# Convolution banks evicted whole and placed by transfers, a one-step candidate in the bisection, and a denser plan of its rounds

## The chip, the core and the metric

One core of a Trainium2 chip runs the whole program. The metric is device time in microseconds of one execution; a kernel is timed by the median of several executions.

## The reference, cut to what matters

The program is one layer of a decoder over 1024 tokens of width 1024. One input projection `x @ w_in` is split by columns into the inputs of three mixers that run side by side:

- sparse attention: a light indexer (8 heads of 32) scores every key for every query, `sum over h of relu(iq_h . ik) * iw_h`; each query keeps its 256 best keys, and softmax attention runs over those;
- a pooling mixer: trailing means over 2, 4, 8 and 16 positions minus the token, then a small linear map;
- a convolution module on 256 channels: `h = a * sigmoid(gate)`, a causal depthwise convolution of width 31 plus bias, a LayerNorm over the 256 channels, then silu.

```python
h = a * jax.nn.sigmoid(gate)
h = lax.conv_general_dilated(h, conv_w, window_strides=(1,), padding=[(CONV_WIDTH - 1, 0)],
                             feature_group_count=D_C, ...) + conv_b
h = layer_norm(h, ln_g, ln_b)
return jax.nn.silu(h)
```

The three outputs are joined, projected with `w_o`, normalised, and pass through a grouped mixture of experts (16 experts, two per token) and a second norm.

## The kernel before, in words

**Stages.** The span has these stretches: load and transposes of x with the first projection units (to about 49 us), the indexer (to about 119), the bisection for the 256th best score (to about 234), attention (to about 396), the output projection, norm and routing (to about 520), the experts, and the last norm.

**Projection units.** The list `UNITS` holds 33 projection units (index 0 to 32), 8 `key` units and 8 `val` units. A projection unit of 512 columns is 24 matmuls (L472 to L474), with operands split into a high and a low part. ACT evicts most units (`unit` in the scalar block, L1047 on); ACT also makes the high part of the next weight tile (L1036), and DVE the low part (L1386, `w_split`). Banks are reused every fourth unit.

**Indexer.** From unit 8 (`kv`) on, PE issues `IDX_PER_UNIT` = 6 score products between the matmuls of each projection unit (`index`, L719 to L733); ACT applies relu (L1090), and DVE adds the eight heads up in `bias` (L1446, L1449) and takes the largest magnitude of a block (L1453). There are 48 products, so units 8 to 18 carry them; unit 18 (`gate0`, second half) carries the last three. The products read `stack_iq` and `stack_ik`, which are put together by transfers: SP issues 4 for `stack_ik` and 8 for the high part of `stack_iq` (L555, behind a wait on DVE's low part of unit 3), and ACT issues 8 for its low part (L1108), each of 96 KB. PE waits for all of them before product 0 (L723).

**Bisection.** 25 rounds. In each, DVE counts the scores below a candidate in blocks 7, 6 and 2 (L1502) and ACT in blocks 5, 4 and 3 (L1119). DVE then forms `passed` (L1517), `spot` (L1519) and the next candidate (L1520); at the head of the next round it forms `floor` (L1497). Both engines take, between their counts, the remaining projection units off a list (`in_round`: 7 units in 10 rounds, unit 19 to 32 in rounds 1 to 19); DVE's part is `w_split` and, for `a0`, the product with the sigmoid (L1432). In the four rounds after these DVE builds the banded weights of the convolution (`toep`, L1511), and ACT evicts two `key` or `val` units in a round.

**Convolution.** The first 128 channels go to PE. Their input is held by time modulo 4 (`phased`), and 16 transfers (L574) stack it. A bank of 256 columns for each of four groups of 32 channels takes `SPAN` = 9 matmuls (L763); `CONV_PER_UNIT` = 3 of them stand before each unit from `CONV_FROM` = 37 on. In a bank, partition 32q + c holds channel c of the group at phase q. `conv_out` (L1123 to L1128) evicts each bank with four ACT instructions of 32x256, which move the phases to the group's 32 partitions and write every fourth element, so that `conv[:, 0, :]` comes out in the order of time. The other 128 channels are done by POOL, tap by tap (L1938 to L1952), from the moment the last `a0` unit is done.

**Attention.** The order of steps is computed by `attention_steps()`. The first scores need all `key` and `val` units evicted (L794 on, `unit_act`); the second pair needs the bisection's end. Two pool matmuls (L851) wait for all of `conv0`. Near its end stand the LayerNorm steps of the convolution: means (`cm`, L857), subtraction (L1614), squares (L1211), variance (L863), scaling (L1623), silu (L1155). The step `split 0` on ACT and the `cm` step on PE wait for POOL's last tap.

Of the kernel before, what the change touches and what calls it, by code (L numbers as in the profile page):

```python
# [71 lines left out]
CONV_PER_UNIT = 3  # L72
IDX_PER_UNIT = 6
# [137 lines left out]
def program(nc, a):  # L211
    ctx = ExitStack()
    with ctx:
# [37 lines left out]
        stack_h = at("stack_h", [P, PHASES, 264], F32, CC)  # L251
        toep_w = at("toep_w", [P, PHASES, 4 * SPAN], F32, CC + 4.25)
# [142 lines left out]
        spot, floor, thr = (ps[:, 3, 8 * i:8 * i + 6] for i in range(3))  # L395
# [31 lines left out]
        toep_in, phased_in = sem("toep_in"), sem("phased_in")  # L427
# [67 lines left out]
        CONV_FROM = PROJECTIONS + 4  # L495
# [14 lines left out]
        def in_round(r):  # L510

            return (r + 1) * 7 // 10 - r * 7 // 10
# [5 lines left out]
        def _(sp):  # L518
# [43 lines left out]
            sp.wait_ge(unit_dve, seen(BY_DVE, UNITS.index(("iq0", 1, 1))))  # L562
# [101 lines left out]
        def _(pe):  # L664
# [88 lines left out]
            def conv_part(n):  # L753
# [14 lines left out]
            for k, between in PLAN[1:]:  # L768
                if k >= CONV_FROM:
                    for n in range(CONV_PER_UNIT):  # L770
                        conv_part((k - CONV_FROM) * CONV_PER_UNIT + n)
# [9 lines left out]
            for step in STEPS:  # L781
                kind = step[0]
                if kind in RING:
                    r = step[-1]
                    out = ps[:, 4 + (r + 2) % 3, :]
                    if r in (1, 2):
                        pe.wait_ge(conv0, PHASES * PHASES)
# [243 lines left out]
        def _(act):  # L1031
# [1081 lines left out]
```

## Time and profile before

| what | us |
|---|---|
| median of 3 executions | 994.54 (991.64 to 996.25) |
| the profiled execution | 993.15 |
| its span in the profile | 991.4 |
| PE busy in the span | 892.1 (90%) |
| DVE busy | 689.7 (70%) |
| ACT busy | 570.5 (58%) |
| POOL busy | 344.9 (35%) |

A row of the timeline gives start, duration, engine, line, operation, output and inputs, shape and count, and in brackets the idle time of the engine before it and who ended that. The chain of waits follows back, from the last instruction, what each piece of work waited for; it lists start, length and work. PE's durations are modelled with a pipelined end, so two matmuls in a row overlap; the distance of their starts, which the chain shows, is what each costs.

### The profile page before, as it was taken

Reading aid. Unit: us, or ns where it says so; the run is one execution under the profiler, and the core shown is the slowest. Engines: PE = TensorE matmul, PEld = TensorE weight load, DVE = VectorE, ACT = ScalarE, POOL = GpSimd, SP = SyncE. Lnnn points to the kernel's source line nnn. Section 1 sums busy time; section 2 is a strip of 40 time slices with the busy share of each in tenths; the row PEclk is TensorE's granted clock in tenths of the full one; section 3 lists DMA queues with packets and bytes.
Section 4 is the critical chain, followed back from the end, with each engine's and each line's share of the span. In section 5 each row is a group of like instructions: output and inputs, shape, how many; then the busy total and the mean of one; then the engine's idle time right before and its main releaser. Section 6 shows DMA issues by size and latency. Waiting matters only on the chain.

```text
span 991.4 us, 15972 instructions
## 1 busy us (share of the span) xinstructions
PE 892.1 (90%) x4780; PEld 714.1 (72%) x4781; DVE 689.7 (70%) x1060; ACT 570.5 (58%) x820; POOL 344.9 (35%) x264
## 2 busy tenths in 40 slices
PE   6999989888899899999918999999999999999980
PEld 5778868655466567888816888888878888888760
DVE  5478799994789945737687757888888854234276
ACT  5276567678787665702233647778777743324342
POOL 0000059999999940000001112132332321111137
PEclk9989989999899999999968999999999999999995
DMA  8731022000000100433576779999999987652475
GB/s 229 189 78 43 22 65 86 1 1 1 1 1 2 43 2 23 152 132 123 229 286 225 248 229 339 380 403 388 397 404 385 400 295 243 185 148 44 108 243 211
DMA packets 64254, 173.08 MB, mean 175 GB/s; under 512 B 19553, under 2 KB 34401, under 8 KB 51888
## 3 DMA queue, kind: packets, MB, share of 16 engines
q1 hardware_dynamic: 56048, 143.61, 39.2%
q0 software_dynamic: 7488, 27.07, 11.1%
q10 hardware_dynamic: 672, 1.84, 0.5%
q8 instruction: 24, 0.39, 0.2%
q14 instruction: 22, 0.18, 0.1%
HBM read 142.79 MB, written 26.74 MB: 171 GB/s over the span
## 4 chain that ended last, share of the span: by engine, by line
PE 59%; DVE 17%; DMA 11%; issue 6%; ACT 5%; ACTq 1%; DVEq 0%; POOLq 0%; POOL 0%; SPq 0%
PE ps L472 14%; PE ps L474 14%; PE ps L473 14%; DMA raw<-in_w_gate 10%; DVE junk_dve L1502 6%; PE ps L806 3%; PE ps L836 3%; PE ps L823 2%; DVE wlo L1809 2%; PE ps L962 2%; PE ps L731 1%; DVE sm L1655 1%; ACT whi L1280 1%; PE ps L763 1%; ACT junk_act L1119 1%
## 5 line engine op out<-in xcount | busy, mean ns | idle before, releaser
L1809 DVE TENSOR_TENSOR wlo<-raw,whi 128x2048 fp32r<-128x2048 f32 x96 | 216.2, 2288 | 51.8 <-ACT whi L1280 51.8
L1280 ACT CAST whi<-raw 128x2048 fp32r<-128x2048 f32 x96 | 180.3, 1911 | 50.2 <-DMA raw<-in_w_gate 17.0
L472 PE MATMUL ps<-whi,xgT_hi 128*128 128x512 f32 x384 | 152.6, 397 | 6.2 <-DVE xgT_lo L1819 6.2
L474 PE MATMUL ps<-whi,xgT_lo 128*128 128x512 f32 x384 | 150.3, 392 | 0.0
L473 PE MATMUL ps<-wlo,xgT_hi 128*128 128x512 f32 x384 | 150.2, 391 | 0.0
L472 PE MATMUL ps<-xT_hi,w_hi 128*128 128x512 f32 (+1 forms) x224 | 89.7, 401 | 8.7 <-DVE w_lo L1386 6.9
L472 PEld LDWEIGHTS ps<-whi,xgT_hi 128*128 128x128 f32 x384 | 72.7, 189 | 22.3 <-issue 6.3
L473 PE MATMUL ps<-xT_lo,w_hi 128*128 128x512 f32 (+1 forms) x224 | 88.4, 395 | 0.0
L474 PE MATMUL ps<-xT_hi,w_lo 128*128 128x512 f32 (+1 forms) x224 | 88.4, 394 | 0.0
L2020 POOL COPY idx_now<-slot_token 128x1 int32 (+1 forms) x24 | 8.2, 343 | 219.3 <-PE ps L962 219.3
L474 PEld LDWEIGHTS ps<-whi,xgT_lo 128*128 128x128 f32 x384 | 72.5, 189 | 15.5
L473 PEld LDWEIGHTS ps<-wlo,xgT_hi 128*128 128x128 f32 x384 | 72.5, 189 | 14.3
L1119 ACT ACTIVATE junk_act<-bias,sm 128x768 bf16<-128x768 f32 (+2 forms) x75 | 62.2, 829 | 27.8 <-DVE sm L1520 25.8
L472 PE MATMUL ps<-whi,hT_hi 128*128 128x512 f32 x192 | 76.9, 401 | 0.5 <-issue 0.5
L1502 DVE TENSOR_SCALAR_CACHE_REDUCE junk_dve<-bias,sm 128x1024 bf16<-128x1024 f32 (+2 forms) x75 | 75.7, 1009 | 1.8
L474 PE MATMUL ps<-whi,hT_lo 128*128 128x512 f32 x192 | 75.1, 391 | 0.0
L473 PE MATMUL ps<-wlo,hT_hi 128*128 128x512 f32 x192 | 74.9, 390 | 0.0
L2035 POOL DMA_INDIRECT acc_d<-ysb,idx_add x23 | 40.6, 1763 | 92.8 <-ACT ysb L1307 91.9
L1590 DVE CUSTOM_DVE_ANT_0 probs<-ps,bias 128x128 f32<-128x128 f32 (+7 forms) x64 | 45.9, 755 | 36.0 <-PE ps L806 30.7
L1948 POOL TENSOR_SCALAR tapped<-hpad,par 128x512 f32<-128x512 f32 x32 | 58.3, 1833 | 0.1
L1297 ACT ACTIVATE silu<-ps 128x512 f32<-128x512 f32 x24 | 14.3, 596 | 76.5 <-PE ps L474 76.5
L472 PEld LDWEIGHTS ps<-xT_hi,w_hi 128*128 128x128 f32 x224 | 43.6, 195 | 18.9 <-issue 8.0
(335 smaller groups left out, 1874.4 us busy)
## 6 DMA issues: line engine op xcount, KB each, us to landing
raw<-in_w_gate SPq DMA_DIRECT2D x32, 1024.0 KB, 12.0
raw<-in_w_up SPq DMA_DIRECT2D x32, 1024.0 KB, 12.7
raw<-in_w_down SPq DMA_DIRECT2D x32, 1024.0 KB
w_raw<-in_w_in SPq DMA_DIRECT2D x14, 512.0 KB, 3.9
x_tok<-in_x SPq DMA_DIRECT2D x8, 512.0 KB, 7.8
wo_raw<-in_w_o SPq DMA_DIRECT2D x16, 256.0 KB, 2.9
x_res<-in_x SPq DMA_DIRECT2D x16, 256.0 KB, 3.5
x_d<-xa SPq DMA_DIRECT2D x4, 512.0 KB, 5.7
```

The costliest lines, as they stand in the source:

```text
L472: pe.matmul(out, l_hi, r_hi, start=start, stop=False)
L473: pe.matmul(out, l_hi, r_lo, start=False, stop=False)
L474: return pe.matmul(out, l_lo, r_hi, start=False, stop=stop)
L806: last = pe.matmul(scores_at(u + h, WIDTH[b])[:, c:c + n], qT[rows, j, b * P:(b + 1) * P], keyT[rows, j, c:c + n], start=True, stop=True)
L836: last = pe.matmul(product_at(pair_no)[h * HD:(h + 1) * HD, :], value[:, k, (2 * j + h) * HD:(2 * j + h + 1) * HD], pT[:, PT_NO[b, j, n] % ...
L1119: act.activation(junk_act[:, 0:WIDTH[b]], bias[:, AT[b]:AT[b] + WIDTH[b]], ACT.Sign, bias=cands[r % 2][:, c:c + 1], scale=-1.0, accum_out= ...
L1280: act.copy(whi[:, n, :], raw[:, n, :]).then_inc(gu_hi if n < 4 else dn_hi, 1)
L1502: dve.tensor_scalar(junk_dve[:, 0:WIDTH[b]], bias[:, AT[b]:AT[b] + WIDTH[b]], now[:, c:c + 1], 0.0, ALU.is_lt, ALU.add, accum_out=res[:, c ...
L1590: dve.tensor_tensor_reduce(out=probs_at(u)[:, 0:WIDTH[b]], in0=scores_at(u, WIDTH[b]), in1=bias[:, AT[b]:AT[b] + WIDTH[b]], scale=-1.0, sc ...
L1809: dve.tensor_tensor(wlo[:, n, :], raw[:, n, :], f32(whi[:, n, :]), ALU.subtract).then_inc(gu_lo if n < 4 else dn_lo, 1)
L1948: pool.tensor_scalar(tapped[:, half], src[:, half], by, None, ALU.mult).then_inc(tap_mul, 1)
L2035: pool.indirect_dma_start(acc_d, bass.IndirectOffsetOnAxis(ap=idx_add[:], axis=0), ysb[:], None, compute_op=ALU.add).then_inc(y_out, 16)
```

## The change

- Indexer: 7 products in a unit in place of 6, so that unit 17 carries the last three and unit 18 moves into the bisection. Of ACT's 8 transfers of the low part, 4 go to the POOL queue, with a semaphore of their own. SP's 8 transfers of the high part wait for ACT's eviction of unit 3, no longer for DVE's low part.
- Bisection: `floor` is carried from round to round, `spot` and the instruction L1497 go; the candidate is `(floor + step / 2) * top_score` in one instruction. Units are taken in 5 rounds of 6, so units 18 to 32 lie in rounds 1 to 17, `toep` in rounds 18 to 21.
- Convolution: 5 matmuls before each unit, from unit 41 on. One ACT instruction of 128x256 evicts a bank into `stepped`; 16 transfers on SP's queue, four for each bank, put it in place. `conv[:, 0, :]` is then held phase-major (all times of one phase together), and the LayerNorm's steps, the squares and the silu read or write it through a rearranged view.

```diff
-CONV_PER_UNIT = 3
-IDX_PER_UNIT = 6
+CONV_PER_UNIT = 5
+IDX_PER_UNIT = 7
...
+        stepped = at("stepped", [P, PHASES, 256], F32, R2 + 28)
...
-        CONV_FROM = PROJECTIONS + 4
+        CONV_FROM = PROJECTIONS + 8
+
+        def conv_ends(k):
+
+            return [g for g in range(PHASES) if (SPAN * (g + 1) - 1) // CONV_PER_UNIT == k - CONV_FROM]
+
+        def conv_at(i, c):
+
+            if i:
+                return conv[:, 1, c * 512:(c + 1) * 512]
+            return conv[:, 0, :].rearrange("p (r v) -> p v r", r=PHASES)[:, c * P:(c + 1) * P, :]
...
-            return (r + 1) * 7 // 10 - r * 7 // 10
+            return (r + 1) * 5 // 6 - r * 5 // 6
...
-            sp.wait_ge(unit_dve, seen(BY_DVE, UNITS.index(("iq0", 1, 1))))
+            sp.wait_ge(unit_act, seen(BY_ACT, UNITS.index(("iq0", 1, 1))))
             stack(0, range(2))
...
+            for g in range(PHASES):
+                sp.wait_ge(conv0, g + 1)
+                for q in range(PHASES):
+                    t0 = (PHASES - 1 - q) * 256
+                    sp.dma_start(conv[g * CH:(g + 1) * CH, 0, t0:t0 + 256], stepped[q * CH:(q + 1) * CH, g, :]
+                                 ).then_inc(phased_in, 16)
             sp.wait_ge(searched, 1)
...
-                    pe.wait_ge(stack_in[0], 16 * 20)
+                    pe.wait_ge(stack_in[0], 16 * 16)
+                    pe.wait_ge(stack_lo_in, 16 * 4)
...
-                        pe.wait_ge(conv0, PHASES * (g - 1))
+                        pe.wait_ge(conv0, g - 1)
...
                     pe.wait_ge(conv1, 2 * TAPS)
+                    pe.wait_ge(phased_in, 2 * 16 * PHASES * PHASES)
                     for i in range(2):
-                        last = pe.matmul(out, ones_conv[:], conv[:, i, c * 512:(c + 1) * 512], start=i == 0, stop=i == 1)
+                        last = pe.matmul(out, ones_conv[:], conv_at(i, c), start=i == 0, stop=i == 1)
...
-                    for part in range(2, 4):
-                        for h4 in range(4):
-                            act.dma_start(f32(stack_iq[part * IDIM:(part + 1) * IDIM, h4, :]),
-                                          f32(iqT_lo[h4 * IDIM:(h4 + 1) * IDIM, 0, :])).then_inc(stack_in[0], 16)
+                    for h4 in range(4):
+                        act.dma_start(f32(stack_iq[2 * IDIM:3 * IDIM, h4, :]),
+                                      f32(iqT_lo[h4 * IDIM:(h4 + 1) * IDIM, 0, :])).then_inc(stack_in[0], 16)
...
                 act.wait_ge(conv0_mm, g + 1)
-                for q in range(PHASES):
-                    act.activation(conv[g * CH:(g + 1) * CH, 0, PHASES - 1 - q::PHASES], conv_bank(g)[q * CH:(q + 1) * CH, :],
-                                   ACT.Identity, bias=phase_bias[q * CH:(q + 1) * CH, g:g + 1]).then_inc(conv0, 1)
+                act.activation(stepped[:, g, :], conv_bank(g), ACT.Identity, bias=phase_bias[:, g:g + 1]).then_inc(conv0, 1)
...
-            dve.memset(spot, 0.0)
+            dve.memset(floor, -1.0)
...
-                dve.tensor_scalar(floor, spot, -step / 2 if r + 1 < ROUNDS else -step, None, ALU.add)
...
-                    link(dve.scalar_tensor_tensor(spot, passed, step, floor, ALU.mult, ALU.add))
-                    dve.tensor_tensor(then, spot, top_score, ALU.mult).then_inc(cand_set, 1)
+                    link(dve.scalar_tensor_tensor(floor, passed, step, floor, ALU.mult, ALU.add))
+                    dve.scalar_tensor_tensor(then, floor, step / 2, top_score, ALU.add, ALU.mult).then_inc(cand_set, 1)
...
-                        ch = conv[:, i, c * 512:(c + 1) * 512]
-                        dve.tensor_tensor(ch, ch, src, ALU.subtract).then_inc(ring_dve if i else conv_c, 1)
+                        ch = conv_at(i, c)
+                        dve.tensor_tensor(ch, ch, src if i else src.rearrange("p (v r) -> p v r", r=PHASES), ALU.subtract).then_inc(ring_dve if i else conv_c, 1)
...
-            pool.wait_ge(stack_in[0], 16 * 20)
+            pool.wait_ge(unit_dve, seen(BY_DVE, UNITS.index(("iq0", 1, 1))))
+            for h4 in range(4):
+                pool.dma_start(f32(stack_iq[3 * IDIM:4 * IDIM, h4, :]),
+                               f32(iqT_lo[h4 * IDIM:(h4 + 1) * IDIM, 0, :])).then_inc(stack_lo_in, 16)
+            pool.wait_ge(stack_lo_in, 16 * 4)
+            pool.wait_ge(stack_in[0], 16 * 16)
```

The squares, the scaling and the silu get rearranged views in the same way. The counts on `toep_in` move to `dve_set`, which changes no order of work.

## Rows read from the trace of the kernel before

**Rows 1.** Busy time by stretch: window, length, PE, PEld, DVE, ACT, POOL, granted clock.
```profile
50.00:119.00 69.00, 66.87 (x305) 55.06 (x304) 53.84 (x64) 45.98 (x63) 3.45 (x8) 0.95 0.20 51
...
143.00:149.00 6.00, 5.83 (x14) 4.62 (x15) 5.66 (x18) 5.37 (x11) 5.68 (x3) 0.50 0.39 106
```

**Rows 2.** Chain of waits: the indexer's end, and the first counts of rounds 0 and 18.
```profile
115.09 0.23 PE ps L472
...
117.33 0.19 PE ps L731
...
119.97 1.20 DVE junk_dve L1502 x2
...
201.16 1.20 DVE junk_dve L1502 x2
```

**Rows 3.** Chain of waits: from the bisection's end to the first softmax row.
```profile
230.36 2.24 PE ps L763 x6
...
235.74 0.86 PE ps L710 x2
236.60 1.30 PE ps L763 x6
...
248.79 1.28 ACT L1190
250.09 0.88 ACT probs L1190 x4
```

**Rows 4.** Timeline around the indexer's start: the queues of SP and ACT, then PE.
```profile
38.09 5.04 SPq L555 DMA_DIRECT2D stack_iq<-iqT_hi  x8
...
39.63 6.43 ACTq L1108 DMA_DIRECT2D stack_iq<-iqT_lo  x8
...
49.37 0.74 PE L731 MATMUL ps<-stack_ik,stack_iq 128*128 128x512 f32 x2 [2.06 <-DMA stack_iq<-iqT_lo]
```

**Rows 5.** Transfers: time of an issue on POOL; median time from issue to landing (last figure).
```profile
L2023 POOL DMA_INDIRECT xg<-x_d,idx_now x24 | 30.9, 1286 | 18.3 <-POOL idx_now L2020 17.5 <-DMA acc_d<-ysb,idx_add 0.8
...
stack_iq<-iqT_lo ACTq DMA_DIRECT2D x8, 96.0 KB, 2.8
...
xg<-acc_d,idx_add POOLq DMA_INDIRECT x1, 4.5
```

**Rows 6.** Bisection: a plain round on DVE; groups of ACT's counts and DVE's banded weights.
```profile
147.37 0.17 DVE L1497 TENSOR_SCALAR ps<-ps 128x6 f32<-128x6 f32 x1
...
151.22 0.17 DVE L1497 TENSOR_SCALAR ps<-ps 128x6 f32<-128x6 f32 x1
151.30 1.27 DVE L1502 TENSOR_SCALAR_CACHE_REDUCE junk_dve<-bias,sm 128x1024 bf16<-128x1024 f32 x1
...
L1119 ACT ACTIVATE junk_act<-bias,sm 128x768 bf16<-128x768 f32 (+2 forms) x75 | 62.2, 829 | 27.8 <-DVE sm L1520 25.8
...
L1511 DVE TENSOR_TENSOR toep<-ps,toep_w 128x1152 f32<-128x1152 f32 x4 | 5.4, 1353 | 0.0
```

**Rows 7.** Evictions on ACT: the convolution's banks, and a contiguous one of 256 columns.
```profile
L1127 ACT ACTIVATE conv<-ps,phase_bias 32x256 f32<-32x256 f32 x16 | 11.5, 718 | 0.4
...
31.28 0.37 ACT L1064 CAST iqT_hi<-ps 128x256 fp32r<-128x256 f32 x1
```

**Rows 8.** DVE products with a strided output (L1432: least/median/most ns) and a plain one.
```profile
L1432 DVE TENSOR_TENSOR hpad<-ps,sig x2: 1121/1124/1127, 127.9 to 132.6; 128x512 f32<-128x512 f32 x2
...
L1437 DVE TENSOR_TENSOR hpad<-ps,sig 128x512 f32<-128x512 f32 x2 | 1.3, 670 | 0.0
```

**Rows 9.** POOL's last work on the convolution, and the chain where it is needed.
```profile
352.91 2.51 POOL L1952 TENSOR_TENSOR conv<-conv,tapped 128x512 f32<-128x512 f32 x2
...
373.05 3.44 PE ps L857 x8
```

**Rows 10.** DVE's small copies between 40 and 43 us.
```profile
L1468 DVE COPY toep_w<-par 32x31 f32<-32x31 f32 x8 | 1.4, 176 | 0.2
```

**Rows 11.** Waits of PE from 119 to 260 us: total, times, longest.
```profile
PE ps L472 <- DVE w_lo L1386: 6.9, 2, 3.8
```

More of the change, by code:

```diff
@@ L393, in pair @@
             return ps[:, 2 * i:2 * i + 2, :].rearrange("p b n -> p (b n)")
-        spot, floor, thr = (ps[:, 3, 8 * i:8 * i + 6] for i in range(3))
+        floor, thr = (ps[:, 3, 8 * i:8 * i + 6] for i in range(2))
         unit_mask = ps[:, 3, P:P + CH]
@@ L769, in _ @@
                 if k >= CONV_FROM:
-                    for n in range(CONV_PER_UNIT):
-                        conv_part((k - CONV_FROM) * CONV_PER_UNIT + n)
+                    for n in range((k - CONV_FROM) * CONV_PER_UNIT, min((k - CONV_FROM + 1) * CONV_PER_UNIT, PHASES * SPAN)):
+                        conv_part(n)
                 unit(k, between)
@@ L786, in _ @@
                     if r in (1, 2):
-                        pe.wait_ge(conv0, PHASES * PHASES)
+                        pe.wait_ge(conv0, PHASES)
                     if r >= 3:
@@ L1125, in conv_out @@
                 act.wait_ge(conv0_mm, g + 1)
-                for q in range(PHASES):
-                    act.activation(conv[g * CH:(g + 1) * CH, 0, PHASES - 1 - q::PHASES], conv_bank(g)[q * CH:(q + 1) * CH, :],
-                                   ACT.Identity, bias=phase_bias[q * CH:(q + 1) * CH, g:g + 1]).then_inc(conv0, 1)
+                act.activation(stepped[:, g, :], conv_bank(g), ACT.Identity, bias=phase_bias[:, g:g + 1]).then_inc(conv0, 1)
             def late_item(k, between):
                 item(k, between)
-                g, part = divmod((k - CONV_FROM + 1) * CONV_PER_UNIT - CONV_PER_UNIT, SPAN)
-                if k > CONV_FROM and part == 0:
-                    conv_out(g - 1)
+                for g in conv_ends(k):
+                    conv_out(g)
             act.wait_ge(masked_s, len(BLOCKS))
-            act.wait_ge(toep_in, 1 + 2 * PHASES * PHASES)
+            act.wait_ge(dve_set, 3 + 2 * PHASES * PHASES)
             for r in range(ROUNDS):
@@ L1154, in mix_split @@
                         for i in range(2):
-                            act.activation(mix[:, 6 + i, :], conv[:, i, :], ACT.Silu, bias=cvb[:, i:i + 1],
-                                           scale=cvg[:, i:i + 1]).then_inc(conv_y, 1)
+                            out = mix[:, 6 + i, :]
+                            if i == 0:
+                                out = out.rearrange("p (v r) -> p r v", r=PHASES)
+                            act.activation(out, conv[:, i, :] if i else conv[:, i, :].rearrange("p (r v) -> p r v", r=PHASES),
+                                           ACT.Silu, bias=cvb[:, i:i + 1], scale=cvg[:, i:i + 1]).then_inc(conv_y, 1)
                         act.wait_ge(conv_y, 2)
@@ L1210, in _ @@
                     for i in range(2):
-                        act.activation(csq[:, i, c * 512:(c + 1) * 512], conv[:, i, c * 512:(c + 1) * 512], ACT.Square
+                        part = csq[:, i, c * 512:(c + 1) * 512]
+                        act.activation(part if i else part.rearrange("p (v r) -> p v r", r=PHASES), conv_at(i, c), ACT.Square
                                        ).then_inc(conv_sq, 1)
@@ L1467, in phase_taps @@
                 for g in range(PHASES):
-                    dve.tensor_copy(toep_w[rows, g, 5 - s:5 - s + TAPS], convw[g * CH:(g + 1) * CH, 0:TAPS]).then_inc(toep_in, 1)
-                    dve.tensor_copy(phase_bias[rows, g:g + 1], convb[g * CH:(g + 1) * CH, 0:1]).then_inc(toep_in, 1)
-            dve.wait_ge(toep_in, 1)
+                    dve.tensor_copy(toep_w[rows, g, 5 - s:5 - s + TAPS], convw[g * CH:(g + 1) * CH, 0:TAPS]).then_inc(dve_set, 1)
+                    dve.tensor_copy(phase_bias[rows, g:g + 1], convb[g * CH:(g + 1) * CH, 0:1]).then_inc(dve_set, 1)
+            dve.wait_ge(dve_set, 3)
             phases = list(range(PHASES))
@@ L1492, in _ @@
             dve.wait_ge(masked_s, len(BLOCKS))
[L1493 removed]
+            dve.wait_ge(dve_set, 3 + 2 * PHASES * PHASES)
             toeps = 0
```

10 lines of the change are left out of this document (4 added, 6 removed).

## The prediction

> **What bounds the kernel now.** I read the table of busy time by stretch first, then the chain of waits over the stretches that the diff touches, then the timelines of the single engines there. Three things are to be seen. The indexer is paced by PE: in its 69 us PE is busy for 66.87, DVE for 53.84 [rows 1], and the chain runs through PE up to the last score product at 117.33 [rows 2]. The bisection is a loop on DVE: the chain goes from count to count, from 119.97 to 201.16 for the first 18 rounds, or 81.2 us [rows 2]. Behind it the chain runs through PE's convolution and value matmuls, then through ACT's evictions of the last bank, a table load at 248.79 and the first softmax row at 250.09 [rows 3]. Everything from there to the end keeps its instructions, apart from the strided views of the LayerNorm. So I work out by how much the point 250.09 moves, and carry that to the end.
>
> **The indexer's start.** PE reaches its first product and waits 2.06 us for ACT's low part of the stack, until 49.37 [rows 4]. ACT's queue took 6.43 us for 8 issues from 39.63; with 4 it takes about 3.2, until 42.9, and with a landing time of 2.8 [rows 5] the data are there at 45.7. The four moved transfers start on POOL at about 38.1, where SP's row starts behind the same wait [rows 4]. No row shows a plain transfer from POOL. From below I take ACT's price (0.8 each, 2.8 to land: 38.1 + 3.2 + 2.8 = 44.1), from above POOL's indirect ones (1.29 an issue, 4.5 to land: 38.1 + 5.2 + 4.5 = 47.8) [rows 5]. PE wants them at 49.37 - 2.06 = 47.3. I take the nearest in kind, POOL's own, with half a microsecond lost at most: the wait goes, -2 us. After a wait PE is granted half its clock for a while (1.2 GHz where it had 2.4; 0.50 over 143 to 149, behind another wait [rows 1]); for about 4 us that costs another 1.5 to 2, which goes as well. Behind POOL's new waits stand its clearing of the bias and the causal masks; these are first needed when a block's scores are summed, some 20 us later, and cost nothing. SP's earlier start of the high part only lets its weight load go sooner: nothing.
>
> **The indexer's length.** Unit 18 leaves it: 24 matmuls at 0.23 [rows 2], 5.5 us of PE. Sum with the start: 9.1 us. PE's gain is not all kept, since DVE now gets 7 products in a unit in place of 6: it has 69 - 53.84 = 15 us of idle time, of which 9 would go [rows 1]. I take 1 us back: the first count moves from 119.97 to about 112 (**-8 us**; from -4.5, if POOL's transfers eat the start, to -9.5).
>
> **The bisection.** Without L1497 a count starts 0.08 us earlier in a round (151.22 to 151.30 [rows 6]); the candidate's instruction changes its form only. That is 1.4 us over 18 rounds: DVE alone would need 79.8 in place of 81.2. But one unit more lies in two rounds fewer. PE starts unit 18 about 2.6 us ahead of the first count (117.33 to 119.97 [rows 2]) and needs 15 x 5.5 = 82.5 us for units 18 to 32, so the last is done 79.9 after the first count, and evicted 0.6 later. The two paths meet: PE loses the slack that it had. I take round 18 at +80.3. DVE's six weight splits remain six. The four rounds with the banded weights cost a plain round (147.37 to 151.22 is 3.85, less 0.08) and up to 1.35 more each [rows 6]; a little of that lies in the wait for ACT's counts, so I take 1.15. That makes 4 x 4.9 = 19.7, and round 22 starts at +100.0. On ACT the three counts (0.83 each [rows 6]) and the reading of their sums take some 2.8; then it evicts two value units (0.5 each) and the first bank whole.
>
> **The evictions.** Sixteen instructions of 0.718, 11.5 us [rows 7], become four of 128x256 with contiguous output. The contiguous one of 256 columns took 0.37 [rows 7]; with a bias column I take 0.4, from above the old 0.718: 1.6 us in all, and 10 us of ACT go. The first bank is out at 100.0 + 2.8 + 1.0 + 0.4 = +104.2.
>
> **The tail.** Matmul 18 of the 36 waits for that bank. Behind it stand 18 convolution matmuls at 1.30 / 3 = 0.43 and 5 value units at 0.86 [rows 3]: 12.0 us. After the wait the clock is low again: three matmul pairs took 2.24 in place of 1.30 [rows 3], and what follows them likewise, so +2. PE is done at +118.2. Then the last value unit is evicted (0.6), the last bank (0.4), and the table load (1.28 [rows 3]) leads to the first softmax row at **+120.5**. In the kernel before that row stands at 250.09 - 119.97 = +130.1: **-9.6 us**. The search itself ends at about +113 and does not decide. The 16 placing transfers are issued on SP behind each bank; the next things in that queue are two small parameter loads, needed by POOL after its last tap, and the output weights, which wait for a later step anyway. Their cover is attention up to the means at 373.05 [rows 9].
>
> **Strided LayerNorm.** DVE's four steps on the phase-major half cost up to 1.124 - 0.670 = 0.45 more each [rows 8], 1.8 in all; the two near the means have PE's products beside them. PE's means (3.44 for eight passes [rows 9]) read half their data in steps of 1 KB. No row shows such a matmul: from below nothing, from above twice the price of four passes, 1.7. The squares and the silu run on ACT beside PE. I take +0.7 in all; the ends are 0 and +3.5. The Trainium skill ("SBUF — State Buffer", section "Door 1: The DMA port swizzle") says that each access to a new 16-byte line pays a penalty, without a figure; by it the sum would lie towards that upper end.
>
> **Sum.** -8 - 9.6 + 0.7 = -17. The profiled execution took 993.15, of which 991.4 is span; that makes 976. It lies 1.4 under the median of 994.54, so for a median I say **977**.
>
> **The rivals.**
> (a) *POOL's transfers come late.* DVE runs 16 small copies in the same 2 us in which POOL would issue. If each issue waited, the four would start near 42.6 and end near 42.6 + 5.2 + 4.5 = 52.3, 3 us after 49.37: the start loses 3 in place of gaining 3.5. Time 983. For it: no plain POOL transfer is in the trace. Against: a copy lasts 0.18 us [rows 10], so that a wait for one is short. The Trainium skill (the same page, section "SBUF: two separate sides") says that descriptors of POOL's transfers can't be written while DVE runs a two-port copy; by that rule the time would be this rival's. Chance 0.14.
> (b) *The half clock and DVE's feeding cost nothing.* Then the start and the tail give 3 to 4 more: 973. The gain ends at POOL: its last tap ends at 355.4, the means need it at 373.05 [rows 9], 17.6 later, and POOL starts about 4 us earlier only, since the last `a0` product moves from round 2 to round 3. So no more than some 22 us, 971, can come of it. Chance 0.15.
> (c) *POOL becomes the bound earlier*, because more of its taps meet DVE's attention work: its taps then end up to 5 us later, and the gain is cut to 14: 980. Chance 0.08.
> (d) *Slower.* PE has no slack in rounds 2 to 17. If DVE's weight split comes late, PE waits (3.8 us at the longest, two waits with 6.9 in sum before [rows 11]), runs at half clock for 5 us after it [rows 1], and that unit's eviction holds up ACT and the next split: 3.8 + 2.5 = 6.3 us for each of the five tiles split in these rounds, 31 in all; 977 + 31 = 1008. It decides from three such waits on (19 us). Against: the split stands two units ahead of its use. Chance 0.03.
> (e) *The change does not do what it says:* the bank's eviction waits for PE as long as ACT worked before, or the transfers hold up the means, and only a few us are left: 990 to 995. Chance 0.03.
> The forecast has 0.57.
>
> **How the numbers follow.** The forecast's own spread is the start (±2), the meeting of DVE and PE (±2), the tail's clock (±2) and the strided views (+2.8), some ±5. With (a), (b) and (c) taken in the range is 969 to 985. Half a per cent, about what a measurement can tell from no change, is 5 us: faster means under 989.6. Faster 0.94 ((a) to (c) and the forecast), same 0.03 (most of (e)), slower 0.03 ((d)).
>
> **What would show it.** Right: the first product without a DMA wait at about 47; the first count at 112; PE without gaps from there to unit 32; four evictions of some 0.4; the first softmax row about 120 after the first count; POOL's last tap still ahead of the means. Wrong: PE waits on the weights' low part, a first product after 50, whole-bank evictions near 0.7, the means waiting on POOL, or attention longer than before.

## The result, and the profile after

The changed kernel takes **986.97 us** (median of 7 runs, 983.33 to 987.99) against 992.19 (7 runs, 988.90 to 996.25) for the kernel before beside it; the ratio is 0.9925, 95% interval 0.9901 to 0.9950. So it is faster, though not by the 17 us forecast: the medians lie 5.2 us apart, and the ratio stands for 7.4 us, with an interval that ends at half a per cent. 977 and the range 969 to 985 are both missed. The profiled execution took 983.33 (span 981.6), the fastest of the seven, against 993.15 before, 9.8 us less. The accounts below are made between these two profiles.

Where the 17 us of the sum should have come from, and what came, by the marks that the prediction set:

| mark | before | forecast | after |
|---|---|---|---|
| first score product | 49.37 | 47 | 47.08 |
| first count | 119.97 | 112 | 117.13 |
| round 18, behind the first count | 81.2 | 80.3 | 80.2 |
| first bank out, behind the first count | | 104.2 | 104.0 |
| first softmax row, behind the first count | 130.1 | 120.5 | 118.8 |
| first softmax row | 250.09 | 232.5 | 235.92 |
| means | 373.05 | | 358.81 |
| squares' matmuls | 389.50 | | 377.27 |
| broadcast of the deviation | 395.55 | | 384.93 |

Two steps failed. The first count moved by 2.8 us in place of 8, and behind the means another 3.6 us were lost (14.2 us of gain at the means, 10.6 at the broadcast) where +0.7 was forecast. What lies between held within 2 us.

**The start** held. The timelines of the queues and of PE (POOL, ACT and PE; as [rows 4]):

```profile
38.67 2.26 POOL L1932 DMA_DIRECT2D stack_iq<-iqT_lo  x4 [36.15 <-DVE iqT_lo L1432]
...
39.57 2.69 ACTq L1127 DMA_DIRECT2D stack_iq<-iqT_lo  x4
...
47.08 0.62 PE L750 MATMUL ps<-stack_ik,stack_iq 128*128 128x512 f32 x2
```

POOL issues four transfers in 2.26 us, 0.57 each and below the lower bound of 0.8, ACT its four in 2.69, and PE's first product waits for nothing. Five profiles with the old transfers have the first product at 49.4 to 51.8, ten with the new ones at 47.1 to 47.9.

**The indexer** did not hold. Two pieces of the chain, from the point where it passes from DVE to PE and from its end (as [rows 2]), then the busy time (as [rows 1]; the second row is a stretch further below):

```profile
97.67 0.81 DVE bias L1468
...
99.81 0.61 ACT relu L1110
...
114.63 0.18 PE ps L750
...
114.84 0.50 ACT relu L1110
...
115.36 0.63 DVE bias L1468
...
116.02 0.56 DVE sm L1472
...
117.13 1.30 DVE junk_dve L1520 x2
```

```profile
47.50:117.00 69.50, 63.69 (x284) 51.19 (x283) 54.62 (x74) 44.95 (x61) 4.04 (x9) 0.95 0.21 54
...
381.00:386.00 5.00, 5.00 (x48) 4.67 (x45) 1.03 (x3) 1.14 (x4) 0.00 (x0) 0.66 0.00 0
```

From the first product to the first count 70.05 us pass (117.13 - 47.08), and 70.6 passed before. PE's busy time did fall, from 66.87 to 63.69, but the length of the stage did not: PE now idles 5.8 us in it. The chain's share by line says who took over. Before, PE's products and projections led (L731, L472 to L474); now DVE's head sum does (L1468). First before, over 49 to 119, then after, over 45 to 118:

```profile
by line: PE ps L731 19.8%; PE ps L472 18.1%; PE ps L473 18.0%; PE ps L474 17.9%; DMA stack_iq<-iqT_lo 7.4%; issue 6.6%; DVE bias L1449 6.1%; ACT relu L1090 4.9%; PE ps L695 2.7%; PE ps L699 2.7%; DVE bias L1446 0.9%; ACT sq L1054 0.9%; DVE 
```

```profile
by line: DVE bias L1468 20.8%; issue 15.0%; SPq L566 11.9%; ACT relu L1110 6.8%; PE ps L750 5.9%; PE ps L475 5.7%; PE ps L473 5.4%; PE ps L474 5.4%; PE ps L713 4.9%; DVE w_lo L1405 3.3%; DMA stack_iq<-iqT_lo 3.0%; DVE bias L1465 2.3%; ACT L
```

So the limit changes hands within the stage: from about 58 to 100 us the chain runs mostly through relus and DVE's sums, and from 100.46 to 114.63 through nothing but PE. Ahead of that it runs through SP's transfers (L566), to which the prediction gave no term: PE now reaches product 8 before the second half of the stack has landed, and waits 1.2 us for it, where the kernel before had no such wait.

```profile
58.09 0.73 PE L750 MATMUL ps<-stack_ik,stack_iq 128*128 128x512 f32 x2 [1.21 <-DMA stack_iq<-iqT_lo]
```

**The tail** held (ACT's timeline, the chain on PE, SP's queue; to be compared with [rows 3, 7]):

```profile
220.67 0.48 ACT L1145 ACTIVATE stepped<-ps,phase_bias 128x256 f32<-128x256 f32 x1
...
234.62 1.28 ACT L1208 ACT_TABLE_LOAD   x1
235.92 0.40 ACT L1208 ACTIVATE probs<-probs,sm 128x128 f32<-128x128 f32 x1
```

```profile
223.26 2.16 PE ps L782 x10
225.42 0.86 PE ps L728 x2
226.28 2.16 PE ps L782 x10
```

```profile
221.18 16.56 SPq L595 DMA_DIRECT2D conv<-stepped  x16
```

An eviction of a whole bank takes 0.48 (0.4 forecast, 0.718 a quarter before), a convolution matmul 0.43 as forecast, and no half clock follows the wait for the first bank (granted clock 1.00 over 216 to 237), for which 2 us had been set. Hence +118.8 in place of +120.5.

**Behind the means** (PE's groups and timeline; to be compared with [rows 9]):

```profile
L877 PE MATMUL ps<-conv,ones_conv 128*128 128x512 f32 x8 | 5.4, 820 | 0.0
```

```profile
377.10 3.73 PE L883 MATMUL ps<-ones_conv,csq 128*128 128x1 f32 x32
380.76 3.53 PE L855 MATMUL ps<-pT,value 128*64 128x128 f32 x32
```

The means take 5.21 us in place of 3.44, which is the upper bound of the forecast. And 32 value products take 3.53 us where the kernel before had 1.97: the clock is at half for a while there (0.66 over 381 to 386, above), which no step of the prediction had.

### The profile page after: what moved, and what is told of

It reads as the page before. It is cut to its first block, busy times and chain, and to the rows that moved or that the text cites. A ratio compares the mean times of both kernels' runs of the same rounds, so it can differ in the third digit from the quotient of the medians.

```text
span 981.6 us, 15954 instructions
## 1 busy us (share of the span) xinstructions
PE 889.8 (91%) x4780; PEld 711.3 (72%) x4781; DVE 688.7 (70%) x1035; ACT 561.3 (57%) x808; POOL 344.4 (35%) x268
## 3 DMA queue, kind: packets, MB, share of 16 engines
q0 software_dynamic: 7616, 27.46, 11.3%
## 4 chain that ended last, share of the span: by engine, by line
PE 56%; DVE 19%; DMA 11%; issue 6%; ACT 6%; SPq 1%; DVEq 0%; ACTq 0%; POOLq 0%; POOL 0%
PE ps L473 14%; PE ps L475 13%; PE ps L474 13%; DMA raw<-in_w_gate 10%; DVE junk_dve L1520 6%; PE ps L825 3%; PE ps L855 3%; PE ps L842 2%; DVE wlo L1827 2%; DVE bias L1468 2%; PE ps L982 2%; DVE tie_no L1558 1%; ACT junk_act L1138 1%; DVE sm L1673 1%; ACT whi L1299 1%
## 5 line engine op out<-in xcount | busy, mean ns | idle before, releaser
L474 PE MATMUL ps<-wlo,xgT_hi 128*128 128x512 f32 x384 | 150.2, 391 | 0.0
L473 PE MATMUL ps<-xT_hi,w_hi 128*128 128x512 f32 (+1 forms) x224 | 87.4, 390 | 2.8 <-DVE xT_lo L1412 1.7
L474 PE MATMUL ps<-xT_lo,w_hi 128*128 128x512 f32 (+1 forms) x224 | 86.1, 385 | 0.0
L475 PE MATMUL ps<-xT_hi,w_lo 128*128 128x512 f32 (+1 forms) x224 | 86.1, 384 | 0.0
L474 PEld LDWEIGHTS ps<-wlo,xgT_hi 128*128 128x128 f32 x384 | 72.5, 189 | 14.3
L474 PE MATMUL ps<-wlo,hT_hi 128*128 128x512 f32 x192 | 74.9, 390 | 0.0
L1844 DVE SCALAR_TENSOR_TENSOR hid<-silu,slot_gate,ps 128x512 f32<-128x512 f32 x24 | 17.9, 744 | 55.0 <-ACT silu L1316 55.0
## 6 DMA issues: line engine op xcount, KB each, us to landing
raw<-in_w_gate SPq DMA_DIRECT2D x32, 1024.0 KB, 10.7
```

Of the source, the lines that this page charges most:

```text
L473: pe.matmul(out, l_hi, r_hi, start=start, stop=False)
L474: pe.matmul(out, l_hi, r_lo, start=False, stop=False)
L475: return pe.matmul(out, l_lo, r_hi, start=False, stop=stop)
```

## The experiments

A first count, a first softmax row and the stretch behind the means are read from one profile of each kernel; these marks repeat better than the whole time does. Four profiles of kernels that are the same up to there have the first count at 116.77 to 118.11, and the first softmax row 118.8 behind it in three of them, 120.5 in the fourth. Differences of about 1 us in the first count are therefore within the spread.

**What paces the indexer.** Four kernels. First, half of DVE's sums left out (heads 1 to 7 sum the first half of the columns; the rest of the sums is missing):

```
+ if h:
+     acc, r = bias[:, AT[b]:AT[b] + WIDTH[b] // 2], relu[:, u % 2, 0:WIDTH[b] // 2]
```

> The changed kernel with DVE's head sums over the first half of each block's columns only (heads 1 to 7; the other half of the sums is left out, so selection and routing differ and times after the search are not compared). DVE's work in the indexer falls from 54.6 to about 35 us. Theory (DVE's sums are what holds PE back): PE is busy nearly throughout and the first count comes at 112 to 114. Rival (PE waits for relus or for the stack instead): 116 or later.

```profile
113.73 1.28 DVE L1522 TENSOR_SCALAR_CACHE_REDUCE junk_dve<-bias,sm 128x1024 bf16<-128x1024 f32 x1 [0.21 <-DVE sm L1511]
```

```profile
47.50:113.00 65.50, 62.05 (x282) 51.05 (x281) 37.62 (x65) 45.08 (x61) 3.06 (x8) 0.95 0.23 58
```

With DVE at 37.62 us of work PE idles 3.5 us in 65.5, and the first count comes at 113.73: DVE's sums held it back. PE's wait for the second half of the stack is longer here (1.8 us for 1.2), so it is not what set the pace. Next, unit 18 back in the indexer:

```
- IDX_PER_UNIT = 7
+ IDX_PER_UNIT = 6
...
- return (r + 1) * 5 // 6 - r * 5 // 6
+ return (r + 1) * 7 // 10 - r * 7 // 10
```

> The changed kernel with six products to a unit again, so that unit 18 is back in the indexer (bisection units 7 in 10 rounds, as before). Theory (in the changed kernel the indexer is paced by the chain product, relu, head sum on DVE, so that PE's 5.5 us of unit 18 fill what would be idle time): the first count stays at 117 to 118.5 (117.13 in the changed kernel), PE busy for 67 of the 70 us. Rival (PE paces the indexer, and something else ate the gain of 5.5): the first count comes at 122 to 123.

```profile
117.74 1.28 DVE L1520 TENSOR_SCALAR_CACHE_REDUCE junk_dve<-bias,sm 128x1024 bf16<-128x1024 f32 x1 [0.21 <-DVE sm L1509]
```

117.74: a unit of 5.5 us on PE costs the stage 0.6 us, and 1.4 in another kernel further below that is the same up to there (118.52). Both are hardly clear of the spread. Third, the same ten units with the products shared out by their width:

```
+ SHARE = [5, 6, 1, 6, 7, 1, 1, 7, 8, 6]
...
- n = 0 if k < LATER else IDX_PER_UNIT if j is not None else 1
+ n = 0 if k < LATER else SHARE[k - LATER] if k - LATER < len(SHARE) else 0
```

> The changed kernel with the products shared out by their width: 5, 6, 1, 6, 7, 1, 1, 7, 8, 6 to the ten units in place of 7, 7, 1, 7, 7, 1, 1, 7, 7, 3; as many units, the same work on every engine. Theory: while the sums are wide DVE needs more than PE in a unit (7 x 1.29 + 0.6 = 9.6 us against 5.5 + 7 x 0.47 = 8.8), at the end PE needs more; shared out by width the two keep step, and the first count comes at 113.5 to 115.5 (117.13 in the changed kernel); product 8 no longer waits for the second half of the stack. Rival (the order of products does not matter, since the second half of the stack or the relu sets the pace): 116.5 to 117.5.

```profile
114.76 1.28 DVE L1521 TENSOR_SCALAR_CACHE_REDUCE junk_dve<-bias,sm 128x1024 bf16<-128x1024 f32 x1 [0.21 <-DVE sm L1510]
```

114.76, with not an instruction more or less, and no wait for the stack's second half. That is 2.4 of the some 5 us that the forecast had missed. The wait that went with it had been 1.2 us, and the run does not part it from the better balance of PE and DVE. Either way, the mean work of a stage says little when the widths in it run from 1024 to 384. Fourth, the transfers as before (eight on ACT, none on POOL, SP behind DVE; ACT's part of the edit):

```
- for h4 in range(4):
-     act.dma_start(f32(stack_iq[2 * IDIM:3 * IDIM, h4, :]), ...
+ for part in range(2, 4):
+     for h4 in range(4):
+         act.dma_start(f32(stack_iq[part * IDIM:(part + 1) * IDIM, h4, :]), ...
```

> The changed kernel with the transfers of the first half of the stack as before: eight on ACT, none on POOL, SP behind DVE. Theory (from the first product on the chain of products, relus and sums has no slack): first product at 49.4 again, then half the clock for some 4 us; the first count moves back to 119 to 120. Rival (the second half of the stack, which lands at 58 either way, sets the pace from product 8 on): the first count stays at 117 to 118.

The first product came at 50.12 behind a wait of 2.47, the first count at 120.55. The moved transfers are worth 3.4 us, more than the 2.8 by which the first count moved in all. From the first product on the stage takes the same 70.4 us.

**What the tail is made of.** The kernel before with the whole-bank evictions, their transfers and the strided LayerNorm alone (the edit against the changed kernel, beside the old transfers and candidate):

```
- CONV_PER_UNIT = 5
- IDX_PER_UNIT = 7
+ CONV_PER_UNIT = 3
+ IDX_PER_UNIT = 6
...
- CONV_FROM = PROJECTIONS + 8
+ CONV_FROM = PROJECTIONS + 4
...
- return (r + 1) * 5 // 6 - r * 5 // 6
+ return (r + 1) * 7 // 10 - r * 7 // 10
```

> The kernel before with the whole-bank evictions, the placing transfers and the strided LayerNorm alone: six products to a unit, old transfers, old candidate, 7 units in 10 rounds, 3 convolution matmuls to a unit. Theory (the tail hangs on when the first bank is out, and PE's work behind it is fixed): first count 120 as before; the four evictions take 0.5 each, the first bank is out 2.2 us earlier and the last one 2.4 shorter, so the first softmax row stands at +123 to +125 behind the first count (+130.1 before, +118.8 in the changed kernel): 5 to 7 of the 11.3 us come from the evictions, the rest from the plan and the candidate. Rival (the evictions are all of it): +119 to +120. Rival (they were hidden by PE): +128 to +130.

First count 120.84, first softmax row 244.22: +123.4, as expected. Of the 5.9 us by which that row is earlier than before, 1.5 are left at the end (span 989.9 against 991.4), since the strided means and a half clock behind the squares stand here too. And the kernel before with the one-step candidate alone:

```
- dve.tensor_scalar(floor, spot, -step / 2 if r + 1 < ROUNDS else -step, None, ALU.add)
...
- link(dve.scalar_tensor_tensor(spot, passed, step, floor, ALU.mult, ALU.add))
- dve.tensor_tensor(then, spot, top_score, ALU.mult).then_inc(cand_set, 1)
+ link(dve.scalar_tensor_tensor(floor, passed, step, floor, ALU.mult, ALU.add))
+ dve.scalar_tensor_tensor(then, floor, step / 2, top_score, ALU.add, ALU.mult).then_inc(cand_set, 1)
```

> The kernel before with the one-step candidate alone. Theory (a loop on DVE, each round shorter by the 0.08 us of the instruction left out): round 18 starts 79.7 to 80.2 behind the first count in place of 81.2, the first softmax row 1 to 2 us earlier; end 1 to 2 us earlier. Rival (PE's units pace the rounds that hold them, so that a shorter DVE chain only waits longer): round 18 at 81 or later, nothing at the end.

First count 122.18 (its start was 2.4 us later, behind a wait of 3.14 for the stack), first softmax row 250.95: +128.8. Round 18 stands at +80.8, between the two theories, and the first softmax row is 1.3 us nearer. DVE's six weight splits took 12.2 us in this execution and 11.5 in the kernel before (the last section says why), so that the 1.3 are what is left after 0.7 of other origin. Of the 11.3 us between first count and first softmax row the evictions bring 6.7, the candidate 1.3; the other 3.3 are put down to the plan, by difference. To split those, six products to a unit with the new pace kept:

```
- IDX_PER_UNIT = 7
+ IDX_PER_UNIT = 6
```

> The changed kernel with six products to a unit, so that unit 18 is back in the indexer, but with the changed pace of 5 evictions in 6 rounds kept. Theory (the indexer has room on PE for unit 18, the rounds have not): first count at 117 to 118.5 as with six products at the old pace; 14 units in place of 15 lie in the rounds, the last in round 16, the banded weights in rounds 17 to 20, the first bank out one round earlier, about 4 us; first softmax row at +114 to +116 behind the first count (+118.8 in the changed kernel, +123.2 with six products at the old pace). Rival (the pace does not count, PE's convolution and value matmuls end where they did): +118 or later.

First count 118.52, first softmax row 233.78, or +115.3 where the same units at the old pace have +123.2 (240.90 - 117.74). So the pace of 5 in 6 is the good half of the new plan; the six weight splits do not explain it, for they took 11.6 us here and 8.5 at the old pace. With six or seven products to every unit, unit 18 would better have stayed in the indexer: the first softmax row is 2.1 us earlier than in the changed kernel. The end was not: 983.42 in one run, because attention lost these 2 us again (124.8 us from the softmax row to the means, 122.7 in the changed kernel, with the granted clock at 0.95 over 260 to 330 where the other has 1.00).

**What was lost behind the means.** The loops of the strided steps turned round, so that SBUF is read in runs of 128 and the PSUM bank is stepped over:

```
- return conv[:, 0, :].rearrange("p (r v) -> p v r", r=PHASES)[:, c * P:(c + 1) * P, :]
+ return conv[:, 0, :].rearrange("p (r v) -> p r v", r=PHASES)[:, :, c * P:(c + 1) * P]
...
- last = pe.matmul(out, ones_conv[:], conv_at(i, c), start=i == 0, stop=i == 1)
+ last = pe.matmul(out if i else out.rearrange("p (v r) -> p r v", r=PHASES), ones_conv[:], conv_at(i, c),
+                  start=i == 0, stop=i == 1)
...
- dve.tensor_tensor(ch, ch, src if i else src.rearrange("p (v r) -> p v r", r=PHASES), ALU.subtract)
+ dve.tensor_tensor(ch, ch, src if i else src.rearrange("p (v r) -> p r v", r=PHASES), ALU.subtract)
```

> The changed kernel with the loops of the strided LayerNorm steps turned round: phase outside, column inside, so that the convolution's half is read and written in runs of 128 elements, and the means' PSUM bank (written by PE, read by DVE) is stepped over in 16 bytes instead; the squares on ACT stay as they are. Theory (the step of 1 KB in SBUF is what PE and DVE pay for): the eight passes of the means fall from 5.21 to 3.4 to 3.8 us, DVE's four steps on that half from 0.85 to 1.10 back to 0.67 to 0.75, and the half clock after the squares' matmuls, which stands in all changed kernels so far (32 value products in 3.3 to 3.7 us where the kernel before had 1.97) goes, if it hangs on the slow means; PE is then 1.5 to 3.5 us earlier at the first output products. Rival (any stepped operand costs this, PSUM as well): the means stay above 5 and nothing moves; a fall of the clock without slow means says that it has another cause.

The groups of PE and DVE, first of the changed kernel, then with the loops turned:

```profile
L1632 DVE TENSOR_TENSOR conv<-conv,ps 128x512 f32<-128x512 f32 x4 | 3.2, 854 | 0.5 <-PE ps L877 0.5
```

```profile
L877 PE MATMUL ps<-conv,ones_conv 128*128 128x512 f32 x8 | 3.6, 592 | 0.0
...
L1633 DVE TENSOR_TENSOR conv<-conv,ps 128x512 f32<-128x512 f32 x4 | 2.5, 682 | 0.0
```

```profile
374.68 4.92 PE L884 MATMUL ps<-ones_conv,csq 128*128 128x1 f32 x32
379.53 3.68 PE L855 MATMUL ps<-pT,value 128*64 128x128 f32 x32
```

The step of 1 KB in SBUF was the whole price of the means: a matmul falls from up to 1052 to 592 ns, a subtraction from 854 in the mean (two of the four are strided) to 682, and PE's means come back to the time that they had before the change. The half clock stayed, and lasted longer, so it does not hang on the slow means. From the first one-column matmul to the thirteenth output product 13.8 us pass (12.2 in the changed kernel, 10.6 before), which eats most of what the means gave back; one run took 980.62. The rest of the search was for its cause: the 12 output products moved between the one-column matmuls, and then, in the best version, only 6 of them.

```
  for t in range(NT):
      ...
+     if t % 2 == 0:
+         projected(0, t // 2, 1)
```

> The changed kernel with the turned loops of the LayerNorm, and the 32 one-column matmuls of the squares laid between the 12 output products that came behind them (the same instructions in another order on PE). Theory (PE's clock falls behind a run of one-column matmuls; 13.8 us passed from the first of them to the thirteenth output product with the turned loops, 10.6 in the profile of the kernel before): without the run the clock stays at 2.4 GHz, and the same work takes 10.6 to 11.3 us. Rival (the clock falls for what lies ahead of them, a wait or the means): 12 to 14 us, with the half clock at the same time as before.

12.6 us to the next output product, and the value products take 1.97 again: the clock held, but PE then waits 1.84 us, since the products that used to cover DVE's next split are spent. That execution's time, 987.3, has another mishap in it: a half clock in the tail (0.92 over 216 to 237, where the changed kernel has 1.00), its last bank 1.7 us later behind the first count, and one more behind that wait, with output products of 0.63 us where 0.39 is usual. The two kernels profiled once more (an earlier attempt at the first ran with all matmuls at 0.68 us, 1815 us in all, and tells nothing):

> The kernel before, profiled once more. Theory (the half clock behind the squares' one-column matmuls is not the change's doing): it shows here too, 12 to 14 us from the first of them to the thirteenth output product (10.6 in the first profile of this kernel, 12.2 in the changed one). Rival (the change causes it): 10.6 again.

> The changed kernel, profiled once more. Theory (the indexer is paced by DVE's sums, whose work does not vary): 69 to 70.5 us from the first product to the first count again, first softmax row +118.5 to +120.5 behind it; means 5.2 to 5.4 us for eight passes; 12 to 14 us from the first one-column matmul to the thirteenth output product. Rival (the profile of the changed kernel was a mishap, and the forecast's steps hold otherwise): 64 to 66 us in the indexer.

The kernel before, in its second profile:

```profile
388.93 3.73 PE L863 MATMUL ps<-ones_conv,csq 128*128 128x1 f32 x32
392.59 1.97 PE L836 MATMUL ps<-pT,value 128*64 128x128 f32 x32
```

The kernel before with the one-step candidate alone:

```profile
388.35 4.80 PE L863 MATMUL ps<-ones_conv,csq 128*128 128x1 f32 x32
393.08 3.68 PE L836 MATMUL ps<-pT,value 128*64 128x128 f32 x32
```

10.6 again in the kernel before, 12.3 again in the changed one, whose marks repeat as well (70.7 us in the indexer, +118.8, 5.37 for the means), so that it was no mishap. But the candidate alone, which touches nothing in this part, has the half clock too (13.8). So it needs neither the strided views nor the placing transfers. But every kernel with a part of the change and the run unbroken has it, the kernel before in neither profile, and what decides between them stays open.

**The parts together.** Eleven units in the indexer with products shared out by width, the new pace, the turned loops and the spread one-column matmuls; then with 6 of the 12 products moved:

```
+ SHARE = [5, 5, 1, 5, 6, 1, 1, 6, 6, 7, 5]
...
- if t % 2 == 0:
-     projected(0, t // 2, 1)
+ if t in (2, 5):
...
+     projected(0, t // 3, 1)
```

> The parts that the runs so far speak for, together: the changed kernel with 11 units in the indexer, their products shared out by width (5, 5, 1, 5, 6, 1, 1, 6, 6, 7, 5), 5 evictions in 6 rounds, turned loops in the LayerNorm, and the one-column matmuls spread. Theory: first count 116 to 117.5, first softmax row +114 to +116 behind it (3 to 6 us ahead of the changed kernel), means -1.8, clock -1.6 to -3: 6 to 10 us below the changed kernel, 975 to 980, ratio to the kernel before 0.983 to 0.988. Rival (each of these gains is swallowed by the next engine's wait, as the indexer's was): 984 to 988, no better than the changed kernel.

> The best version so far with only 6 of the 12 output products laid between the one-column matmuls, the other 6 behind the broadcast of the deviation again. With all 12 ahead PE waited 1.83 us for DVE's split of the next mix, so that 12.6 us passed to the thirteenth product. Theory (the clock holds with two breaks in the run, and the 6 products cover 1.4 us of that wait): 11 to 11.6 us; about 1 us below the version with 12. Rival (two breaks are not enough): the clock falls again, 12.5 to 14 us, and the time is the same or above.

The first took 980.41 (6 runs, 976.61 to 981.41), ratio to the kernel before 0.9838 [0.9803, 0.9872]; the second **976.41** (974.76 to 978.53), 0.9799 [0.9771, 0.9827]. Both lie below the changed kernel's 0.9925 and outside its interval.

The first missed its expected first count, 116 to 117.5: it came at 118.54, 71.3 us behind the first product, with PE busy for 67.9 of 70.8 us (47.2 to 118). With ten units shared out by width that stretch had been 67.3 us. So once the products are shared out, unit 18 does cost the indexer about 4 us of its 5.5; and as these come back in the bisection, the first softmax row stands at 233.57 with eleven units and at 233.59 with ten. Where unit 18 lies then makes no difference to that row.

The second is not better for the reason given: two breaks were too few, the clock fell (the value products take 3.61), and 12.9 us pass behind the squares. It is better in the bisection, whose first softmax row stands at +111.7 and not at +115.0, and the reason is a single group: rounds 8, 10 and 13, which hold splits, are shorter by 0.88, 1.31 and 1.73 us, round 12 is 0.67 longer, and the others agree. DVE's weight splits in the rounds, first in the version with 12 products moved, then in that with 6 (in the changed kernel they are 11.6 us as well):

```profile
L1413 DVE TENSOR_TENSOR w_lo<-w_raw,w_hi 128x1024 fp32r<-128x1024 f32 x6 | 11.6, 1936 | 0.0
```

```profile
L1413 DVE TENSOR_TENSOR w_lo<-w_raw,w_hi 128x1024 fp32r<-128x1024 f32 x6 | 7.7, 1279 | 0.0
```

The six cost 11.6 or 7.7 us with the same shapes; the last section says why. Six runs with a spread of 4 us speak for the last version, but some 3 us of its lead over the first hang on where the splits fall, which nothing in it controls. The spans of the two profiles differ by 6.2 us; another 3.5 of these arise in the experts, whose code is the same in both, and stay unexplained.

## Why the prediction was right and wrong

**The start: right.** The first product moved by 2.3 us (2 forecast), and with the old transfers the rest of the kernel has its first count 3.4 later (2 + 1.5 to 2 forecast). Rival (a), POOL's transfers late, did not come: four issues in 2.26 us. But it was hardly put to the test, for the prediction had the two in the same 2 us, and DVE's 16 copies ran from 40.42 to 42.55, POOL's issues from 38.67 to 40.93: four copies began beside them. The Trainium skill's rule behind it ("SBUF — State Buffer", section "SBUF: two separate sides") cost nothing that this run shows, and the run says little on it.

**The indexer's length: wrong, and it is the step that failed the forecast.** "Unit 18 leaves it: 24 matmuls at 0.23 [rows 2], 5.5 us of PE", of which "I take 1 us back". The runs took 4 to 5 of the 5.5 back: 0.6 us, in a second run 1.4, lie between six and seven products to a unit. I had weighed DVE's 53.84 us of work against 69 us of stage, and called the remainder idle time to be filled. But a unit with seven products of 1024 columns asks 7 x 1.29 + 0.6 (half a weight split) = 9.6 us of DVE and 5.5 + 7 x 0.47 = 8.8 of PE, while the last unit's three narrow products leave DVE waiting for PE; and between product, relu and sum there are only two buffers, so that I take it that work cannot be saved up from one end for the other (no run has more buffers). The mean hid that the limit changes hands inside the stage. Halving the sums gave 3.4 us, sharing the products out by width 2.4, and with the products shared out unit 18 was worth 3.8 (114.76 against 118.54): the work removed did count, but only where DVE let PE use it. A wait of 1.2 us for the stack's second half had no term either. Of the -8 there remained -2.8, all of it the start's.

**The bisection and the tail: right**, +80.2 for +80.3, +99.9 for +100.0, +104.0 for +104.2. Two terms erred against each other: the eviction 0.48 for 0.4, and the 2 us of half clock in the tail, which did not come (and came in one other kernel). The gain of 11.3 for 9.6 is that term. That "six remain six" holds for the splits, 11.5 us before and 11.6 after, but by luck: in the other kernels here the same six took 7.7 to 12.2.

**The strided LayerNorm: right in kind, wrong in size.** The means cost the upper bound, 1.8 for 1.7, and not the middle. The sentence on the Trainium skill, that by its penalty for each new 16-byte line the sum would lie towards the upper end, was the better guide (a matmul took up to 1052 ns for 592); I should have taken that end, since a step of 1 KB meets a new line with every element. The 1.6 us of half clock behind the squares were not in the sum at all; which part of the change brings them no run shows.

**The sum:** -2.8 - 11.3 + 1.8 + 1.6 = -10.7, which is the broadcast's 10.6, and -9.8 at the end of the span; the 0.8 between them was not traced. -17 was forecast. (b) was half right, for the half clock cost little, but the indexer did not yield what it counted on. (c) and (d) did not come: POOL ended its taps 4.5 us before the means needed them (the row below ends at 354.32, the means start at 358.81), and PE waited 1.1 us for weights in place of 6.9 [rows 11].

```profile
351.83 2.49 POOL L1975 TENSOR_TENSOR conv<-conv,tapped 128x512 f32<-128x512 f32 x2
```

The chances were as wrong as the sum: the range took its spread from the start, the clock and the views, and gave the indexer's step, the largest term with a counter-argument of one line, no case of its own in which DVE takes over at once.

## What to carry to other kernels

Before work is taken off the engine that paces a stage, set the engines against each other unit by unit, not by their sums over the stage: with widths that fall along the way the limit can pass to another engine in the first half and come back in the second. Removing work from one engine pays only as far as the other keeps up: here seven products to every unit gained 0.6 to 1.4 us over six, and as many units with the products shared out by the slower engine's need another 2.4. Where data has to be read in another order, put the step on the side where it is free, here PSUM, before paying for it in SBUF.

## What the hardware showed that was not expected

**A stepped PSUM operand cost nothing, a stepped SBUF operand up to 1.8 times.** A matmul that reads SBUF in steps of 1 KB took up to 1052 ns, one that writes PSUM in steps of 16 bytes 592, a plain one 590. The Trainium skill ("SBUF — State Buffer", section "Door 1: The DMA port swizzle") says that any non-contiguous access to PSUM slows matmuls much; the run with the turned loops does not agree for this write.

**The same split on DVE takes 1.22 to 3.24 us, by what POOL is doing.** Three of the changed kernel's rows on DVE, and POOL's beside them:

```profile
150.60 3.24 DVE L1405 TENSOR_TENSOR w_lo<-w_raw,w_hi 128x1024 fp32r<-128x1024 f32 x1
161.17 1.22 DVE L1405 TENSOR_TENSOR w_lo<-w_raw,w_hi 128x1024 fp32r<-128x1024 f32 x1
169.72 1.60 DVE L1405 TENSOR_TENSOR w_lo<-w_raw,w_hi 128x1024 fp32r<-128x1024 f32 x1
```

```profile
150.36 2.39 POOL L1966 TENSOR_TENSOR conv<-conv,tapped 128x1024 f32<-128x1024 f32 x1
...
159.28 2.85 POOL L1964 TENSOR_SCALAR tapped<-hpad,par 128x1024 f32<-128x1024 f32 x1 [0.17 <-POOL conv L1966]
...
167.84 2.40 POOL L1966 TENSOR_TENSOR conv<-conv,tapped 128x1024 f32<-128x1024 f32 x1
```

The split that starts beside POOL's sum of two SBUF operands ends 1.09 us after that sum does (153.84 against 152.75), the third 1.08 after (171.32 against 170.24). So it stood still until POOL's instruction was over. In fourteen profiles of this case every split that begins while such a sum runs ends 1.07 to 1.11 us behind it. Beside POOL's scaling of one operand it depends on the moment: the second split, 1.9 us into a scaling, loses nothing, but in seven profiles one that begins 0.09 to 0.32 us behind a scaling's start takes 1.87 to 2.11 us. The best version has the reverse. First the version with 12 products moved, then that with 6:

```profile
156.95 2.85 POOL L1972 TENSOR_SCALAR tapped<-hpad,par 128x1024 f32<-128x1024 f32 x1 [0.17 <-POOL conv L1974]
...
157.04 2.10 DVE L1413 TENSOR_TENSOR w_lo<-w_raw,w_hi 128x1024 fp32r<-128x1024 f32 x1
```

```profile
157.06 3.92 POOL L1972 TENSOR_SCALAR tapped<-hpad,par 128x1024 f32<-128x1024 f32 x1 [0.17 <-POOL conv L1974]
...
157.13 1.22 DVE L1413 TENSOR_TENSOR w_lo<-w_raw,w_hi 128x1024 fp32r<-128x1024 f32 x1
```

DVE starts 0.09 us behind POOL in the one and waits, 0.07 behind in the other and does not, and POOL's scaling takes 3.92 us in place of 2.85. The Trainium skill ("SBUF — State Buffer", section "Who interferes with whom") calls the pair of ports that both use an exclusive lock. The rows with POOL's sums agree; a scaling held a split up only near its start, and the split ended 2.2 us after that start, before the scaling did, which a lock kept to the scaling's end would not give. From this split on the two loops meet at other moments, and three of the six splits are shorter, 3.9 us in all.

**A run of one-column matmuls can leave PE at half clock though the profile shows no wait in it:** behind 32 of them the value products took 2.9 to 3.7 us for 1.97 in 11 of 15 profiles (granted clock 0.66 over 381 to 386 in the changed kernel). Four breaks of wide products went with the full clock in both kernels that had them, two did not; the kernel before keeps it without any, in both its profiles, so that the run of one-column matmuls alone does not decide it.
